# Rounding every weight tile on ScalarE in a two-layer hybrid decoder step

## The reference

```python
def _layer(x, pos, st, p, lb):
    z = jnp.einsum('btd,dp->btp', x, w_in)            # 15 groups of 512 columns, and 8 gate columns
    hA, ... = _mlstm_chunked(q_a, k_a * DH_A ** -0.5, v_a, i_a + b, log_sigmoid(f_a + b), C0, n0, m0)
    yA = sigmoid(o_a) * _head_rms(hA, norm_a)
    hB, ... = _retention_chunked(rope(q_b), rope(k_b) * DH_B ** -0.5, v_b, log_gamma, Sr0)
    yB = silu(g_b) * _head_ln(hB, norm_b)
    kc = (1 - lb) * sigmoid(-f_c)
    hC, ... = _gla_chunked(silu(q_c), kc, i_c, log1p(-min(kc, clamp)), Sh0)
    yC = silu(g_c) * _head_rms(hC, norm_c)
    yD = bg_d * conv3(cg_d * x_d)
    proj = jnp.einsum('btnw,nwd->btnd', stack([yA, yB, yC, yD]), w_branch)
    gates = sigmoid(x @ w_gate + b_gate)
    mix = jnp.sum(gates * proj, axis=2) @ w_out
    h = _layer_norm(ALPHA * x + mix, ln1_g, ln1_b)
    out = _layer_norm(ALPHA * h + square(relu(h @ w_up)) @ w_down, ln2_g, ln2_b)
```

## Time and profile before

| | |
|---|---|
| Time, median of 3 runs | 1632.7 us (1632.21 to 1633.67) |
| The profiled execution: its time | 1634.62 us |
| The profiled execution: its span, first to last instruction | 1632.8 us |
| Mean granted TensorE clock | 0.975 |
| Matmuls, instructions | 10450 of 25994 |
| Read from and written to HBM | 206.33 MB, 15.58 MB, 136 GB/s over the span |

### The profile page before, as it was taken

One profiled execution on the slowest core, in us unless ns is written; L12 is line 12 of the kernel. 1 busy time (PEld: TensorE's weight loads), 2 busy tenths in 40 slices (PEclk: granted clock), 3 DMA queues, 4 the chain that ended last, 5 costly groups with the idle time before them and its releaser, 6 DMA issues.

```text
span 1632.8 us, 25994 instructions
## 1 busy us (share of the span) xinstructions
PE 1547.6 (95%) x10450; PEld 1483.6 (91%) x10450; DVE 927.1 (57%) x1727; ACT 653.4 (40%) x1190; POOL 900.8 (55%) x391
## 2 busy tenths in 40 slices
PE   7899999999999889999898999999999997999997
PEld 7899989998999789999888999889899996999996
DVE  4874774256866854422447748643477668544224
ACT  5434443344434343433344344343444433433233
POOL 6555453444455557666754554444445455566764
PEclk9999999999999989999999999999999999999999
DMA  8333443333545334444433335433345353354442
GB/s 278 116 116 117 164 167 118 121 128 118 171 144 161 112 93 153 149 150 149 135 105 115 117 104 198 145 114 122 118 149 167 106 166 94 116 152 147 154 144 83
DMA packets 66256, 223.60 MB, mean 137 GB/s; under 512 B 8024, under 2 KB 12632, under 8 KB 66136
## 3 DMA queue, kind: packets, MB, share of 16 engines
q1 hardware_dynamic: 66136, 221.93, 42.4%
HBM read 206.33 MB, written 15.58 MB: 136 GB/s over the span
## 4 chain that ended last, share of the span: by engine, by line
PE 84%; DVE 11%; ACT 2%; issue 2%; DMA 1%; SPq 0%; DVEq 0%; ACTq 0%
PE gps L1207 24%; PE gps L1208 23%; PE gps L1209 23%; PE xp L1433 2%; PE xp L1370 1%; PE xp L1435 1%; DVE mix L940 1%; PE xp L1348 1%; DVE rs L1099 1%; DMA raw<-in_w 1%; PE xp L1422 1%; DVE mix L828 1%; PE xp L1329 1%; PE xp L1339 1%; DVE mix L1134 1%
## 5 line engine op out<-in xcount | busy, mean ns | idle before, releaser
L570 POOL TENSOR_TENSOR wlo<-raw,whi 128x1024 fp32r<-128x1024 f32 x362 | 879.7, 2432 | 703.8 <-ACT whi L591 432.6
L1207 PE MATMUL gps<-xh,whi 128*128 128x320 f32 x2000 | 644.4, 322 | 43.3 <-DVE xl L1144 22.7
L1208 PE MATMUL gps<-xl,whi 128*128 128x320 f32 x2000 | 626.7, 313 | 0.0
L1209 PE MATMUL gps<-xh,wlo 128*128 128x320 f32 x2000 | 626.4, 313 | 0.0
L591 ACT ACTIVATE whi<-raw 128x1024 fp32r<-128x1024 f32 x258 | 273.0, 1058 | 501.7 <-PE gps L1209 447.6
L1207 PEld LDWEIGHTS gps<-xh,whi 128*128 128x128 f32 x2000 | 384.1, 192 | 51.7 <-issue 29.6
L1208 PEld LDWEIGHTS gps<-xl,whi 128*128 128x128 f32 x2000 | 384.2, 192 | 3.2 <-issue 0.4
L1209 PEld LDWEIGHTS gps<-xh,wlo 128*128 128x128 f32 x2000 | 383.3, 192 | 0.0
L1207 PE MATMUL gps<-ah,whi 128*128 128x320 f32 x640 | 200.5, 313 | 0.6
L1208 PE MATMUL gps<-al,whi 128*128 128x320 f32 x640 | 198.7, 310 | 0.0
L1209 PE MATMUL gps<-ah,wlo 128*128 128x320 f32 x640 | 198.7, 310 | 0.0
(11 more groups left out here) (279 smaller groups left out, 1827.3 us busy)
## 6 DMA issues: line engine op xcount, KB each, us to landing
raw<-in_w SPq DMA_DIRECT2D x362, 512.0 KB, 3.6
s<-in_st SPq DMA_DIRECT2D x24, 512.0 KB, 4.5
out_ss<-s SPq DMA_DIRECT2D x24, 512.0 KB, 2.7
con<-in_cst SPq DMA_DIRECT2D x4, 526.0 KB, 6.1
out_sp<-pst SPq DMA_DIRECT2D x24, 64.0 KB, 2.6
mix<-in_x SPq DMA_DIRECT2D x4, 320.0 KB, 5.6
out_y<-mix SPq DMA_DIRECT2D x8, 160.0 KB, 1.9
ee<-in_cst SPq DMA_DIRECT2D x1, 224.0 KB, 4.8
```

The costliest lines, as they stand in the source:

```text
L570: nc.gpsimd.tensor_tensor(wlo[:, c % RING, :, :], raw[:, c % RING, :, :], whi[:, c % RING, :, :].bitcast(F32), ALU.subtract).then_inc(lo_d ...
L1207: M(out, hi, xhi, start=start, stop=False)
L1208: M(out, hi, xlo, start=False, stop=False)
L1209: return M(out, lo, xhi, start=False, stop=stop)
```

## The change

`hi_engine` gives "act" for all tiles. The copy of 128 x 1024 behind a sigmoid slot is then an ACTIVATE on ScalarE in ACT's order, and DVE has no `split_hi` any more; POOL waits for ACT's semaphore throughout. Nothing else is edited. The values don't change in kind: the rounding is the one that the other tiles have.

```diff
 def hi_engine(c):
 
-    return "dve" if c >= RING and sigmoids(SLOTS[(c - RING) % NSLOT]) else "act"
+    return "act"
```

## The result

| | before | after |
|---|---|---|
| median of 4 runs each, us | 1633.2 (1632.2 to 1636.2) | 1667.1 (1665.9 to 1671.7) |
| ratio, 95% interval | | 1.0216 (1.0201 to 1.0231) |
| profiled execution, span of core 0, us | 1632.8 | 1664.1 |

A forecast was written before the change was run, and what follows sets the result against it. TensorE, busy for 95% of the span, and its waits were taken as the bound. Terms summed to 6.3 us a layer, 12.6 for both, plus 1.7 for clock: 1632.7 + 14.3 = 1647.0 us; eight-in-ten range 1638 to 1657.

The forecast's parts named there:

- Rival 4: Every copy shows: the 0.32 us price difference in all 104 slots, 33 us, 1666 us; chance 0.02.
- `c_log` and `c_first`: Where DVE and ACT alternate and PE waits, POOL starts earlier and periods shorten: -2.6 us a layer.
- `fin` B: Four B heads, `b_mean` to `fin`: ACT's square comes later, PE waits 0.72 us each, +2.9 us a layer.
- `num` A0 and A3: ACT's `seen` copy comes later and PE waits for it: +0.97 and +0.8 us a layer.
- `num` C3: ACT stands before a late weight load, `seen` comes later and PE waits: +1.55 us a layer.
- Last gates of B: Behind gate B3 ACT, not DVE, waits for the load, delaying L851 and branch tiles: +1.0 us a layer.
- `fin` A0: Behind C's last gate ACT is 0.97 us later, but DVE's L1021 no longer meets POOL: +0.4 us a layer.
- `a_cum`: Late load delays ACT's copy and PE's transposes, +1.9 us a layer; a wait at L851 two slots on shrinks, -0.8.
- The clock: New long waits bring PE one more stretch at its lower clock: +1.7 us for the program.
- `b_rope` in front of its scores: Added cost at the `b_rope` stage ahead of its scores: 0.2 us a layer, bounds 0 to 0.4.
- POOL and the weights: POOL's subtraction starts 0.36 us later in the slot, hidden by over 3 us before PE needs the weights: nothing.
- Rival 3: Slower still: waits feed each other through late weight loads and bring lower-clock stretches, 1656.1 us; chance 0.20.

The follow-up runs named there:

- e13: The change with ScalarE's copy behind Abs, Exp and Ln in the sigmoid slots and POOL's subtraction in four quarters: 1606.9 us, 0.9833 of the kernel before.
- e12: The kernel before with POOL's subtraction in four quarters, no copy moved: 1606.3 against 1634.1 us, ratio 0.9838.
- e3: The change with ScalarE's copy behind Abs, Exp and Ln in the sigmoid slots instead of ahead of them: 1.0155 of the kernel before.
- e7: The change with SyncE sending the outputs of fin and conv and the next state's load one slot later: 1.0216 of the kernel before.
- e4: The change with a one-column memset where DVE's cast stood, for which POOL's subtraction waits too: 1649.9 against 1631.5 us for the kernel before.
- e9: The kernel before with POOL's subtraction in two halves, nothing else: 1611.3 against 1633.5 us, ratio 0.9869.
- e10: The kernel before with ScalarE rounding also behind qC and gC, there behind Ln, and POOL's subtraction in four quarters: 1599.2 against 1633.5 us.
- e1: The kernel before with ScalarE rounding also behind the sigmoid tiles of fC, qC and gC only: 1624.5 against 1631.5 us, ratio 0.9957.

## Why the prediction was wrong

*The shares and the kind of bound* were right: ACT has 45% and does not set the pace (e13, with all copies on ScalarE, is as fast as e12), and the moved busy time counts for nothing by itself. Rival 4's 33 us a program came out by number, 34, and not by mechanism: it wanted 0.32 us in each of 104 slots, and the steady gate slots keep their pitch; the loss sits in some 20 places a layer, of 0.2 to 2.5 us each.

*`c_log` and `c_first`, -2.6 a layer.* The period of L940 became 5.02 us, as worked out (its ends after: 65.42, 70.44, 75.45), and slot 18 starts 2.4 us earlier in layer 0 and 2.7 in layer 1, counted from the layer's first dense matmul. By pitch the stretch gained 3.4 a layer, and fC's slots gave 0.5 back, since the copy delays Abs there as well, a cost that the forecast didn't have.

*`fin` B, +2.9 a layer*, measured +3.4: each of the eight is 0.85 us, not 0.72. The order of causes was as told, and e3 took all of it away. *`num` A0 and A3, 0.97 and 0.8:* right, 3.8 for both layers against 3.5. *`num` C3, +1.55*, measured 1.15, with the load as the greater part (e7). *Last gates of B, +1.0*, measured 1.4. *`fin` A0, +0.4:* 0.9 and 0.5 in the two layers, and another 0.5 each at `fin` A3 stood in no term. *`a_cum`, +1.9 and -0.8:* in layer 0 as told, a wait of 1.8 us ahead of L1385 after ScalarE had stood 4.5 us before the load, and 0.65 given back two slots on; in layer 1 that wait did not come, and PE waits 2.8 us for L851 two slots on instead, 2.1 more than before. *The clock, +1.7*, measured +3.1. These terms hold in the main.

*The step that failed* is "`b_rope` in front of its scores: 0.2 (0 to 0.4)", and with it the sentence "*POOL and the weights* ... That cover hides the 0.36 us: nothing". It asked only when PE needs POOL's result. It did not ask what POOL shuts out while it makes it, although the paragraph on `c_first` says in the same text that DVE's operations on SBUF are shut out while POOL works. The cast's place in DVE's order tied POOL's start to the end of DVE's stage; without it POOL starts after ScalarE's copy, wherever DVE is then. `b_rope` measured 4.5 us a layer instead of 0.2, and conv with `a_gate`, where the forecast had only a late load (+1.9 and -0.8 a layer), 3.8 instead of 1.1. Of the 5.4 us that conv and `a_gate` cost beyond the forecast, 4.3 lie in the one gap ahead of L1379, where PE had waited 2.5 us in two times before and the prediction had no term. e4 puts both groups back by POOL's start alone, 16.1 of 16.7 us; in these is the 1.8 us of `a_cum`, since the load, too, was waited for less there (2.5 us by ScalarE instead of 4.5).

*The range* ended at 1657. Rival 3 had put 1656.1 on waits that feed each other through late loads, 11 us short of the result; e7 shows that this loop carries 1.7 us at `num` C3 and nothing in the median. The bound for `b_rope` was too narrow. One instruction of DVE that is shut out for one subtraction costs up to 2.4 us, less what hides it. There are eight such stages in the program, so an estimate at half that price would have added some 9 us to the upper side.

*The rule* (the Trainium skill, Perfetto Trace Analysis, Optimizing Scalar/DVE Operations) that DVE with a performance mode is the faster engine agrees with the prices, 0.74 against 1.06 us, and doesn't tell where the loss sits; in e13 the same copies come out even. The same section of the Trainium skill recalls that GpSimd and DVE share a port. Read against the earlier trace rows, that reminder was the one to work out for every stage that POOL can now reach.

## What to carry to other kernels

An instruction that is moved off an engine also takes away an ordering: whoever waited for it (here POOL) now starts at another time relative to the engine's other work. Before moving one, list who waits for it, and what that one shuts out while it runs. Where POOL and DVE work on SBUF side by side, cutting POOL's long operation into four was worth more (28 us, e12) than any choice of engine for the rounding, and a one-column memset as a gate (17 us, e4) does what the cast had done unasked.

## What was not expected of the hardware

- A DVE instruction that works on SBUF alone is held until POOL's running instruction is over, whatever its own size: a copy of 128x2 took 2.36 us instead of 0.16, 128x320 additions 2.58 instead of 0.49. With halves it is 1.47, with quarters 0.92 (e12). The price follows POOL's instruction, not DVE's.
- A DVE instruction with one operand in PSUM is not held. In the kernel before, 116 of them start while a subtraction still has 0.6 us or more to go, and none takes longer than without one; of those on SBUF alone 81 are held, and only four MEMSETs, which read nothing, are not. In e9 L849 (`mix<-mix,gps`) takes 0.49 us at 532.15, while a subtraction runs from 531.89 to 533.27; L831 beside it, with both operands in SBUF, takes 1.47. The Trainium skill (SBUF — State Buffer, SBUF: two separate sides) tells of one port pair that DVE and GpSimd lock for a whole instruction, which DVE wants in a two-port mode or with two SBUF inputs. Both rows agree with it, and so does the price by instruction.
- Cutting is cheap: 2.43 us whole, 2.67 in two, 3.1 in four pieces, the longer ones with DVE's turns in between. POOL was busy for 1101 us instead of 901, and PE waited 0.3 us for it (e10).
- The stretches at the lower clock move with every shift of the schedule. e1 gains 3.3 of its 8.7 us in them, outside C; e7 pays 9.9, e9 gains 5.7. So the sum of a single trace is good to some 5 us, while a group's gap repeats (`fin` B: 6.8 or 6.9 us in all six kernels that have ScalarE's copy ahead of Abs there).

Open stays which waits decide where PE's clock falls, and whether `num` of A0 and A3 would lose their 3.8 us if the copy stood behind `seen` too: no run moved it there.
